# States of two convolutions stored value by value from their channel layout, instead of through transpositions and row transfers

## The chip, the cores and the metric

The kernel runs on one core of a Trainium2 chip. The time is that of one execution on the device in microseconds (us), as the median of three runs. A core has five engines that run side by side, each with its own queue of instructions: TensorE (PE: matrix products and transpositions, results in PSUM), VectorE (DVE), ScalarE (ACT), GpSimd (POOL) and SyncE (SP). ACT, POOL and SP also issue transfers between SBUF and DRAM; 16 DMA engines carry them out. The rows call the queue of SP's transfers q1, that of ACT's q10 and that of POOL's q0. The engines wait for each other by semaphores: a counter that one raises and another waits for.

## The reference

One step of a hybrid decoder layer for two groups of tokens: a prompt (1 sequence of 1024 tokens) and samples (8 sequences of 4 tokens), D_MODEL = 1024, branch width W = 512. What matters here is what two causal convolutions leave behind as their new state:

```python
def causal_dwconv(x, hist, w):
    k = w.shape[0]
    xp = jnp.concatenate([hist.astype(x.dtype), x], axis=1)
    y = lax.conv_general_dilated(xp, w[:, None, :], window_strides=(1,), padding='VALID', ...)
    return y, xp[:, -(k - 1):]

a = a_val * jax.nn.sigmoid(a_gt)
a, new_hist_a = causal_dwconv(a, hist_a, a_dw_w)          # k = 31: 30 rows
ch, new_hist_c = causal_dwconv(c_c * c_h, hist_c, c_conv_w)  # k = 3: 2 rows
```

The outputs touched are new_conv_a_prompt (30 rows of 512 values), new_conv_c_prompt (2 rows of 512), new_conv_a_sample (8 sequences of 30 rows: 26 rows are the old state moved up by 4, and 4 are new) and new_conv_c_sample (8 sequences of 2 rows). All values are 4-byte floats. The rest (three mixers, gates, an output projection, a mixture of 32 experts) is unchanged.

## The kernel before

The prompt is worked in two halves of 512 tokens, g = 0 and g = 1; the 32 sample tokens ride with g = 1 (so 544 columns). Channels lie on the 128 partitions: W = 512 channels are CW = 4 chunks, D_MODEL = 1024 are KD = 8 chunks. A product is an "item": the weight tile of 128 output channels against all tokens, as three products of rounded high parts and low rests (`item`, L2612 to L2614), with g = 1 in two column parts of 272. Items alternate between the PSUM tiles z[0] and z[1].

For each item SP loads the weights into one of WS = 5 buffers (L1308), ACT writes the high part (`w_round`, L1577) and DVE the rest (`w_low`, L1865), AHEAD = 3 items ahead of PE. Everything is written out by hand: each engine's order is the order of the code in its block.

The stretch around the change, in g = 1: after the items of the mixers come 8 pairs of items for the gates of branch C ("GC"), 8 for branch B ("GB") and 8 for branch A ("GA"). A pair is a gate item into z[0] and a branch item into z[1]. ACT takes the sigmoid of z[0] into `sig` (`gate`, L1755) and then rounds two weight tiles; DVE multiplies z[1] by `sig` into `macc`, and between these it does the steps of the convolution over `conv` (L2034), which are all done before the pair GB 3. PE may write z[0] anew when ACT's sigmoid has read it, and z[1] when DVE has multiplied it.

The last rows of the convolutions' inputs are kept by DVE in `a_tail` (128 partitions x 4 chunks x (30 + 32) values: 30 prompt positions, then 8 sequences of 4) and `p_tail` (2 + 32 values), with the channel on the partition. DVE wrote the last of them by 617.1 us, before GC begins. In the outputs the channel is the fastest index, so one partition's values lie 2048 bytes apart in DRAM. Before, they get there like this, all in g = 1:

- PE, after the item GB 0 of h: `states` transposes chunk by chunk into the PSUM tiles q[0] ("stA") and q[1] ("stC"), 16 transpositions (L2503), then `factor_columns` ("mc") transposes `bn_g` into q[0], for which ACT must have read stA.
- ACT, after its four roundings `act1_hi`: four copies out of q into `p_in`, `cv`, `ot[0]`, `ot[1]` (L1773, L1774).
- POOL: a DRAM-to-DRAM transfer of the 26 old rows (L1505), then it waits until ACT has read both, and issues 18 row transfers (L1508 to L1512), each row of 2048 bytes in one piece. Behind them in its queue are the loads of `xres` (L1517).

`st_out` counts these transfers; ACT waits for all of them before its first output item, because `ot` is then overwritten, and POOL before it loads rows into `xA` and `xs_s` (L1532).

Of the kernel before, what the change touches and what calls it, by code (L numbers as in the profile page):

```python
# [80 lines left out]
def build(nc, x_prompt, x_sample, c_prompt, c_sample, state_conv_a, state_conv_c, norm1_g, norm2_g,  # L81
# [5 lines left out]
    with ctx:  # L87
# [375 lines left out]
        def use(s, *name):  # L463
            QFILL[name], QUSE[name] = (s, qn[s]), (s, qf[s])
            qn[s] += 1
            qf[s] += name[0] not in ("ada", "rows")
# [9 lines left out]
        for g in range(2):  # L476
            if g:
                for i in range(PT):
                    use(0, "h2T", 0, i)
            for i in range(CW):  # L480
                use(0, "vT", g, i)
            for t in range(PT + g):
                use(t % 2, "sp", g, t)
            if g:
                use(0, "stA"), use(1, "stC"), use(0, "mc"), use(1, "sc")
            for c in range(CW):
                use(c % 2, "mu", g, c)
            use(1, "var", g)
            if g:
                use(0, "sr")  # L490
            for c in range(CW):
                use(c % 2, "bc", g, c)
            if g == 0:
                for t in range(PT + 1):
                    use(t % 2, "xT", 1, t)
            else:
                use(1, "rank0")
            for n in range(KD):
                use(n % 2, "oT", g, n)
# [211 lines left out]
        def moe_gpsimd(pool):  # L711
# [59 lines left out]
                    pool.wait_ge(m_y, n_)  # L771
                    scatter_dma(0, xcol[:, 0:1], o_sc)

            pool.wait_ge(st_out, 16 * (3 + 2 * NS))

        def step_T(pe, b, s):

# [581 lines left out]
        def _(pool):  # L1359
# [138 lines left out]
            for g in range(2):  # L1498
                if g == 1:

                    pool.wait_ge(vn_ok, 2 * PT + 1)
                    pool.dma_start(new_v_sample[0].rearrange("n t c -> (n t) c"), v_tok[0:SMP, PT, :]).then_inc(v_out, 16)
                    pool.dma_start(bn_g[:, 0:P], modc_dram[0:P, :]).then_inc(mc_in, 16)
                    pool.dma_start(bn_g[0:2 * KD, P:2 * P], modc_dram[P:9 * 2 * KD, :]).then_inc(mc_in, 16)
                    pool.dma_start(new_a_sample[0, :, 0:HA - TS, :], state_conv_a[0, :, TS:HA, :]).then_inc(st_out, 16)  # L1505
                    q_wait_read(pool, "stA")
                    q_wait_read(pool, "stC")
                    pool.dma_start(new_a_prompt[0, 0], p_in[0:HA, 0:W]).then_inc(st_out, 16)  # L1508
                    pool.dma_start(new_c_prompt[0, 0], ot[0][0:HC, 0:W]).then_inc(st_out, 16)
                    for n in range(NS):  # L1510
                        pool.dma_start(new_a_sample[0, n, HA - TS:HA, :], cv[n * TS:(n + 1) * TS, 0:W]).then_inc(st_out, 16)
                        pool.dma_start(new_c_sample[0, n], ot[1][n * TS + TS - HC:(n + 1) * TS, 0:W]).then_inc(st_out, 16)  # L1512
                    pool.wait_ge(v_out, 16)

                pool.wait_ge(blo_ok, CW * (g + 1))
# [10 lines left out]
                pool.dma_start(A2[:], mod_dram[0:1, 4 * D:5 * D].to_broadcast([P, D])).then_inc(ab_in, 16)  # L1526
                if g:
                    pool.wait_ge(alo_ok, 2 * CW)
                    pool.wait_ge(st_out, 16 * (3 + 2 * NS))
                    for k, off in enumerate((3, 4)):  # L1530
                        for n in range(NS):
                            pool.dma_start(xs_s[n * TS:(n + 1) * TS, :] if k else xA[SMP + n * TS:SMP + (n + 1) * TS, PT, :],  # L1532
                                           mod_dram[1 + n:2 + n, off * D:(off + 1) * D].to_broadcast([TS, D])
                                           ).then_inc(abs_in, 16)
# [8 lines left out]
        def _(act):  # L1543
# [129 lines left out]
            for g in range(2):  # L1673
# [72 lines left out]
                for i in range(CW):  # L1746
                    b_chunk(i)


                def gate(n0, i):  # L1750

# [6 lines left out]

                for i in range(KD):
                    gate(GC0, i)  # L1760

                if g == 0:
                    for s in range(2):
# [3 lines left out]
                act.wait_ge(bb_ok, PT + g * (PT + 1))  # L1767
                for c in range(CW):
                    act.activation(act1_hi[:, c, 0:T], u_sb[:, c, 0:T], ACT.Copy).then_inc(bhi_ok, 1)
                if g:  # L1770
                    for k, rows in ((0, HA), (1, HC)):
                        s = q_wait_ready(act, ("stA", "stC")[k])
                        act.activation((p_in, ot[0])[k][0:rows, 0:W], q[s][0:rows, 0, :], ACT.Copy)  # L1773
                        act.activation((cv, ot[1])[k][0:SMP, 0:W], q[s][0:SMP, 1, :], ACT.Copy).then_inc(q_free[s], 1)  # L1774

                def squares(cs):

# [51 lines left out]

                macc_high(KD - 1)  # L1830
                if g:
                    act.wait_ge(st_out, 16 * (3 + 2 * NS))
                for j in range(KD // 2):
                    for s in range(2):
                        if g == 0:
# [663 lines left out]
        def _(pe):  # L2499
# [236 lines left out]
            for g in range(2):  # L2736
# [77 lines left out]
                        spatial(PT, SMP)  # L2814
                    pairs(GC0, i, i + 1, act0_hi, act0_lo)

                def states():
                    for name, src, n in (("stA", a_tail, HA), ("stC", p_tail, HC)):
                        s = q_wait_free(pe, name)
                        for c in range(CW):  # L2820
                            transposed(q[s][0:n, 0, c * P:(c + 1) * P], src[:, c, 0:n])
                            last = transposed(q[s][0:SMP, 1, c * P:(c + 1) * P], src[:, c, n:n + SMP])
                        last.then_inc(q_ready[s], 1)

                def mean(c):
                    s = q_wait_free(pe, "mu", g, c)
                    pe.wait_ge(cnv_ok, g + 1)
# [24 lines left out]

                item(g, GB0, h_hi, h_lo)
                if g:
                    states()
                    factor_columns()
                item(g, GB0 + 1, act1_hi, act1_lo, split_ok=blo_ok)
                pairs(GB0, 1, 3, act1_hi, act1_lo)
# [87 lines left out]
```

## Time and profile before

| | |
|---|---|
| median of 3 runs | 1657.01 us (1656.86 to 1657.71) |
| profiled execution | 1660.13 us, of it span 1658.4 us |
| PE busy | 1584.3 us, 96% of the span |
| DVE, ACT, POOL busy | 1244.5, 808.0, 226.4 us |
| granted PE clock | 0.982 of full over the span |

The span runs from the first to the last recorded instruction. "Busy" sums the instructions of an engine; register, semaphore and DMA-issuing instructions are not counted as busy. A row of the timeline has the start in us, the duration in us (of all instructions merged in it), the engine, the line in the kernel, the operation, the output and input by name, their shapes, the count, and in brackets how long the engine sat idle before it and who released it. ACTq, SPq and POOLq are the parts of these engines that issue transfers.

### The profile page before, as it was taken

How to read it: one execution, taken by the hardware profiler on the slowest of the kernel's cores; microseconds unless marked ns; L12 is line 12 of the kernel's file. 1: busy time of each engine (PE TensorE's matmuls, PEld its weight loads, DVE VectorE, ACT ScalarE, POOL GpSimd, SP SyncE). 2: the span in 40 equal slices, each digit the busy share in tenths (PEclk: the TensorE clock that was granted, in tenths of full speed). 3: DMA queues.
4: the chain of work that ended last, by engine and by line, in shares of the span. 5: the costliest groups of instructions: out<-in, count | busy, mean ns of one | idle time of the engine just before them, and what ended most of it. 6: DMA issues, size and time to landing. Idle time of an engine off the chain costs nothing.

```text
span 1658.4 us, 23365 instructions
## 1 busy us (share of the span) xinstructions
PE 1584.3 (96%) x9186; PEld 1353.4 (82%) x9186; DVE 1244.5 (75%) x1685; ACT 808.0 (49%) x877; POOL 226.4 (14%) x238
## 2 busy tenths in 40 slices
PE   5999999999999999999999989999999999999953
PEld 3777788788789999999999968888888888888841
DVE  4668886746838898877455468898898898898838
ACT  4222232234323213223142367788788788788722
POOL 3310000000000000002000204433212112112100
PEclk9999999999999999999899999999999999999987
DMA  9965222424435222234123648999999999999864
GB/s 341 311 193 167 85 84 83 146 75 143 126 89 168 87 83 81 77 91 135 58 77 102 223 185 302 412 400 395 392 385 377 380 375 383 376 390 396 297 242 179
DMA packets 215984, 368.65 MB, mean 222 GB/s; under 512 B 15266, under 2 KB 163826, under 8 KB 190522
## 3 DMA queue, kind: packets, MB, share of 16 engines
q1 hardware_dynamic: 198972, 332.41, 56.5%
q0 software_dynamic: 16256, 32.58, 5.6%
q10 hardware_dynamic: 646, 2.15, 0.3%
q8 instruction: 74, 1.21, 0.3%
q14 instruction: 36, 0.29, 0.0%
HBM read 353.59 MB, written 31.27 MB: 232 GB/s over the span
## 4 chain that ended last, share of the span: by engine, by line
PE 86%; DVE 8%; DVEq 2%; DMA 2%; issue 1%; ACT 1%; POOL 0%; SPq 0%; POOLq 0%; ACTq 0%
PE z L2612 15%; PE z L2614 15%; PE z L2613 15%; PE z L791 7%; PE z L789 7%; PE z L790 7%; PE z L806 4%; PE z L807 4%; PE z L808 4%; PE q L780 2%; PE q L2503 1%; DMA ada_h<-in_w_ada_dram 1%; PE q L2522 1%; PE q L797 1%; DVE conv L2034 1%
## 5 line engine op out<-in xcount | busy, mean ns | idle before, releaser
L1113 DVE TENSOR_TENSOR wl<-wr,whr 128x2048 fp32r<-128x2048 f32 x198 | 444.0, 2284 | 0.0
L2612 PE MATMUL z<-h_hi,w_hi 128*128 128x272 f32 (+1 forms) x1248 | 409.7, 328 | 3.5 <-DVE h_lo L1865 2.4
L2614 PE MATMUL z<-h_hi,w_lo 128*128 128x272 f32 (+1 forms) x1248 | 404.2, 324 | 0.0
L2613 PE MATMUL z<-h_lo,w_hi 128*128 128x272 f32 (+1 forms) x1248 | 403.3, 323 | 0.0
L952 ACT ACTIVATE whr<-wr 128x2048 fp32r<-128x2048 f32 x198 | 376.3, 1914 | 31.2 <-PE z L791 30.0
L1865 DVE TENSOR_TENSOR w_lo<-w_raw,w_hi 128x1024 fp32r<-128x1024 f32 (+1 forms) x168 | 179.4, 1068 | 135.3 <-ACT w_hi L1577 135.1
L2612 PEld LDWEIGHTS z<-h_hi,w_hi 128*128 128x128 f32 x1248 | 236.3, 189 | 33.7 <-issue 13.4
L2614 PEld LDWEIGHTS z<-h_hi,w_lo 128*128 128x128 f32 x1248 | 236.0, 189 | 17.0
L2613 PEld LDWEIGHTS z<-h_lo,w_hi 128*128 128x128 f32 x1248 | 236.4, 189 | 15.5 <-issue 0.2
L789 PE MATMUL z<-whr,xTh 128*128 128x512 f32 x528 | 208.8, 396 | 0.1
L791 PE MATMUL z<-wl,xTh 128*128 128x512 f32 x528 | 206.1, 390 | 0.0
L790 PE MATMUL z<-whr,xTl 128*128 128x512 f32 x528 | 205.5, 389 | 0.0
L2034 DVE SCALAR_TENSOR_TENSOR conv<-a_in,parT,conv 128x512 f32<-128x512 f32 x360 | 193.7, 582 | 14.1 <-issue 0.9
L1577 ACT ACTIVATE w_hi<-w_raw 128x1024 fp32r<-128x1024 f32 (+1 forms) x168 | 150.4, 929 | 45.0 <-DMA w_raw<-in_w_in_dram 44.9
L1755 ACT ACTIVATE sig<-z 128x512 f32<-128x512 f32 (+1 forms) x48 | 29.3, 611 | 293.4 <-PE z L2614 293.4
L733 POOL DMA_INDIRECT y_rows<-ysb,tb x32 | 78.1, 2442 | 410.9 <-ACT ysb L944 410.9
L791 PEld LDWEIGHTS z<-wl,xTh 128*128 128x128 f32 x528 | 99.1, 188 | 21.2
L789 PEld LDWEIGHTS z<-whr,xTh 128*128 128x128 f32 x528 | 99.6, 189 | 19.8 <-DVE xTl L1113 0.3
L790 PEld LDWEIGHTS z<-whr,xTl 128*128 128x128 f32 x528 | 99.3, 188 | 19.6
L806 PE MATMUL z<-whr,gTh 128*128 128x512 f32 x264 | 105.8, 401 | 0.6 <-DVE gTl L1113 0.6
L808 PE MATMUL z<-wl,gTh 128*128 128x512 f32 x264 | 103.1, 390 | 0.0
L807 PE MATMUL z<-whr,gTl 128*128 128x512 f32 x264 | 103.0, 390 | 0.0
(431 smaller groups left out, 2172.9 us busy)
## 6 DMA issues: line engine op xcount, KB each, us to landing
wr<-in_w_dram SPq DMA_DIRECT2D x198, 1024.0 KB, 9.6
w_raw<-in_w_in_dram SPq DMA_DIRECT2D x104, 512.0 KB, 3.8
ada<-in_w_ada_dram SPq DMA_DIRECT2D x6, 2048.0 KB, 14.1
w_raw<-in_w_branch_dram SPq DMA_DIRECT2D x48, 256.0 KB, 2.7
w_raw<-in_w_out_dram SPq DMA_DIRECT2D x16, 512.0 KB, 4.0
yin<-y_rows SPq DMA_DIRECT2D x16, 512.0 KB, 9.4
ada_h<-in_w_ada_dram SPq DMA_DIRECT2D x2, 2048.0 KB, 15.1
ada_u<-in_w_ada_dram SPq DMA_DIRECT2D x2, 2048.0 KB, 9.8
```

Source lines behind the costliest of these rows:

```text
L789: pe.matmul(out, xTh[s][:, k, :], hi[:, i * FF:(i + 1) * FF], start=(k == 0), stop=False)
L790: pe.matmul(out, xTl[s][:, k, :], hi[:, i * FF:(i + 1) * FF], start=False, stop=False)
L791: last = pe.matmul(out, xTh[s][:, k, :], lo[:, i * FF:(i + 1) * FF], start=False, stop=(k == KD - 1))
L806: pe.matmul(out, gTh[:, k, :], hi[:, w0:w0 + 512], start=(k == 0), stop=False)
L808: last = pe.matmul(out, gTh[:, k, :], lo[:, w0:w0 + 512], start=False, stop=(k == KF - 1))
L952: act.activation(whr[n % HN][:], wr[n % RN][:], ACT.Copy).then_inc(m_hi, 1)
L1113: return dve.tensor_tensor(out, a, b, op)
L1865: return dve.tensor_tensor(out, a, b, op)
L2034: last = dve.scalar_tensor_tensor(out, x, wt, out, ALU.mult, ALU.add)
L2612: pe.matmul(out, w_hi[w][:, k, :], hi[:, k, t0:t1], start=(k == 0), stop=False)
L2613: pe.matmul(out, w_hi[w][:, k, :], lo[:, k, t0:t1], start=False, stop=False)
L2614: last = pe.matmul(out, w_lo[w][:, k, :], hi[:, k, t0:t1], start=False, stop=(k == kn - 1))
```

## The change

The 16 transpositions of PE, the four copies of ACT and POOL's 19 transfers are left out, with the two uses of the q tiles. Instead ACT issues transfers straight from `a_tail` and `p_tail`, one chunk of 128 channels after each of the gates GC 0 to GC 3, with patterns in which every value of 4 bytes goes to its own place in DRAM. The old rows' DRAM-to-DRAM transfer goes to ACT too. `st_out` counts 33 transfers instead of 19; its two waits stay.

```diff
@@ the table of the uses of the q tiles @@
             if g:
-                use(0, "stA"), use(1, "stC"), use(0, "mc"), use(1, "sc")
+                use(0, "mc"), use(1, "sc")
@@ POOL, g == 1 @@
                     pool.dma_start(bn_g[0:2 * KD, P:2 * P], modc_dram[P:9 * 2 * KD, :]).then_inc(mc_in, 16)
-                    pool.dma_start(new_a_sample[0, :, 0:HA - TS, :], state_conv_a[0, :, TS:HA, :]).then_inc(st_out, 16)
-                    q_wait_read(pool, "stA")
-                    q_wait_read(pool, "stC")
-                    pool.dma_start(new_a_prompt[0, 0], p_in[0:HA, 0:W]).then_inc(st_out, 16)
-                    pool.dma_start(new_c_prompt[0, 0], ot[0][0:HC, 0:W]).then_inc(st_out, 16)
-                    for n in range(NS):
-                        pool.dma_start(new_a_sample[0, n, HA - TS:HA, :], cv[n * TS:(n + 1) * TS, 0:W]).then_inc(st_out, 16)
-                        pool.dma_start(new_c_sample[0, n], ot[1][n * TS + TS - HC:(n + 1) * TS, 0:W]).then_inc(st_out, 16)
                     pool.wait_ge(v_out, 16)
@@ ACT @@
+                def states(c):
+                    cc = slice(c * P, (c + 1) * P)
+
+                    def state(dst, src):
+                        act.dma_start(dst, src, allow_slow_non_contiguous=True).then_inc(st_out, 16)
+
+                    if c == 0:
+                        act.dma_start(new_a_sample[0, :, 0:HA - TS, :], state_conv_a[0, :, TS:HA, :]).then_inc(st_out, 16)
+                    state(new_a_prompt[0, 0, :, cc].rearrange("h p -> p h"), a_tail[:, c, 0:HA])
+                    state(new_c_prompt[0, 0, :, cc].rearrange("h p -> p h"), p_tail[:, c, 0:HC])
+                    for t in range(TS):
+                        state(new_a_sample[0, :, HA - TS + t, cc].rearrange("n p -> p n"), seqs(a_tail[:, c, HA:HA + SMP])[:, :, t])
+                    for t in range(HC):
+                        state(new_c_sample[0, :, t, cc].rearrange("n p -> p n"),
+                              seqs(p_tail[:, c, HC:HC + SMP])[:, :, TS - HC + t])
...
                 for i in range(KD):
                     gate(GC0, i)
+                    if g and i < CW:
+                        states(i)
...
-                if g:
-                    for k, rows in ((0, HA), (1, HC)):
-                        s = q_wait_ready(act, ("stA", "stC")[k])
-                        act.activation((p_in, ot[0])[k][0:rows, 0:W], q[s][0:rows, 0, :], ACT.Copy)
-                        act.activation((cv, ot[1])[k][0:SMP, 0:W], q[s][0:SMP, 1, :], ACT.Copy).then_inc(q_free[s], 1)
...
                 if g:
-                    act.wait_ge(st_out, 16 * (3 + 2 * NS))
+                    act.wait_ge(st_out, 16 * (1 + 8 * CW))
@@ PE @@
-                def states():
-                    for name, src, n in (("stA", a_tail, HA), ("stC", p_tail, HC)):
-                        s = q_wait_free(pe, name)
-                        for c in range(CW):
-                            transposed(q[s][0:n, 0, c * P:(c + 1) * P], src[:, c, 0:n])
-                            last = transposed(q[s][0:SMP, 1, c * P:(c + 1) * P], src[:, c, n:n + SMP])
-                        last.then_inc(q_ready[s], 1)
...
                 item(g, GB0, h_hi, h_lo)
                 if g:
-                    states()
                     factor_columns()
                 item(g, GB0 + 1, act1_hi, act1_lo, split_ok=blo_ok)
```

The order of PE before, at the end of the gate item GB 0 in g = 1 (the first column is the instruction's place in PE's row, w_hi and w_lo are the weights' parts):

```order
3852 L2614 MATMUL z<-h_hi_65,w_lo_89 128x272
3853 L2503 MATMUL q<-ident,a_tail 30x128 [waits q_free0]
3854 L2503 MATMUL q<-ident,a_tail 32x128
...
3861 L2503 MATMUL q<-ident,p_tail 2x128 [waits q_free1]
3862 L2503 MATMUL q<-ident,p_tail 32x128
...
3869 L2503 MATMUL q<-ident,bn_g 128x128 [waits mc_in,q_free0]
3870 L2503 MATMUL q<-ident,bn_g 128x16
3871 L2612 MATMUL z<-act_hi_78,w_hi_100 128x272 [waits blo_ok,z_free1,wlo_ok]
```

And now, at the same place:

```order
3852 L2619 MATMUL z<-h_hi_65,w_lo_89 128x272
3853 L2508 MATMUL q<-ident,bn_g 128x128 [waits mc_in,q_free0]
3854 L2508 MATMUL q<-ident,bn_g 128x16
3855 L2617 MATMUL z<-act_hi_78,w_hi_100 128x272 [waits blo_ok,z_free1,wlo_ok]
3856 L2618 MATMUL z<-act_lo_80,w_hi_100 128x272
```

The 16 transpositions from `a_tail` and `p_tail` are gone, and `bn_g` follows the gate item at once; the wait for q_free0 is now for an earlier reader of q[0].

ACT's order before, from the gate GC 0 to GC 2 in g = 1:

```order
285 L1755 ACTIVATE sig<-z 128x544 [waits z_free1,item_mm]
286 L1577 ACTIVATE w_hi_96<-w_raw_91 128x512 [waits w_in0]
287 L1577 ACTIVATE w_hi_97<-w_raw_92 128x1024 [waits w_in1]
288 L1755 ACTIVATE sig<-z 128x544 [waits z_free1,item_mm]
289 L1577 ACTIVATE w_hi_98<-w_raw_93 128x512 [waits w_in2]
290 L1577 ACTIVATE w_hi_99<-w_raw_94 128x1024 [waits w_in3]
```

And now:

```order
285 L1763 ACTIVATE sig<-z 128x544 [waits z_free1,item_mm]
286 L1569 ACTIVATE w_hi_96<-w_raw_91 128x512 [waits w_in0]
287 L1569 ACTIVATE w_hi_97<-w_raw_92 128x1024 [waits w_in1]
288 L1748 DMA out_dram<-in_state_conv_a_dram 8x13312
289 L1745 DMA out_dram<-a_tail 128x30x1
290 L1745 DMA out_dram<-p_tail 128x2x1
291 L1745 DMA out_dram<-a_tail 128x8x1 x4
292 L1745 DMA out_dram<-p_tail 128x8x1 x2
293 L1763 ACTIVATE sig<-z 128x544 [waits z_free1,item_mm]
294 L1569 ACTIVATE w_hi_98<-w_raw_93 128x512 [waits w_in2]
295 L1569 ACTIVATE w_hi_99<-w_raw_94 128x1024 [waits w_in3]
296 L1745 DMA out_dram<-a_tail 128x30x1
```

Nine transfers stand between the sigmoids of GC 0 and GC 1, and eight after each of GC 1, GC 2 and GC 3. None of them waits for a semaphore. POOL's order loses the rows between the load of `bn_g` and the loads of `xres`.

## Rows read from the trace of the kernel before

**Rows 1.** The page: busy time and share of PE, and the chain's shares by engine.
```profile
PE 1584.3 (96%) x9186; PEld 1353.4 (82%) x9186; DVE 1244.5 (75%) x1685; ACT 808.0 (49%) x877; POOL 226.4 (14%) x238
...
PE 86%; DVE 8%; DVEq 2%; DMA 2%; issue 1%; ACT 1%; POOL 0%; SPq 0%; POOLq 0%; ACTq 0%
```

**Rows 2.** Busy by stage: PE, PEld, DVE, ACT, POOL, clock, DMA share, GB/s.
```profile
676.00:712.00 36.00, 34.60 (x299) 33.88 (x298) 33.41 (x73) 8.36 (x12) 2.10 (x4) 1.00 0.32 93
712.00:732.00 20.00, 20.00 (x178) 19.49 (x177) 14.53 (x26) 4.18 (x6) 0.00 (x0) 1.00 0.26 75
...
760.00:800.00 40.00, 40.00 (x312) 37.91 (x311) 29.90 (x57) 7.35 (x11) 11.19 (x23) 1.00 0.45 133
```

**Rows 3.** Timeline of PE at the transpositions.
```profile
755.91 1.03 PE L2503 MATMUL q<-ident,a_tail 128*30 128x128 f32 x8
756.78 1.04 PE L2503 MATMUL q<-ident,p_tail 128*2 128x128 f32 x8
758.10 0.49 PE L2503 MATMUL q<-ident,bn_g 128*128 128x128 f32 x2 [0.28 <-ACT cv L1774]
```

**Rows 4.** Timeline of ACT and DVE from 753 to 787 us, and PE's first mean.
```profile
756.98 0.59 ACT L1773 ACTIVATE p_in<-q 30x512 f32<-30x512 f32 x1 [5.63 <-PE q L2503]
...
758.90 0.60 ACT L1755 ACTIVATE sig<-z 128x544 f32<-128x544 f32 x1
...
753.93 2.62 DVE L1865 TENSOR_TENSOR act_lo<-u_sb,act_hi 128x544 fp32r<-128x544 f32 x4
...
776.26 6.85 DVE L2034 SCALAR_TENSOR_TENSOR conv<-a_in,parT,conv 128x512 f32<-128x512 f32 x14
...
786.71 0.86 PE q L2828 x2
```

**Rows 5.** Timeline of ACT at the gates GC 0 to GC 4.
```profile
676.96 0.63 ACT L1755 ACTIVATE sig<-z 128x544 f32<-128x544 f32 x1 [2.92 <-PE z L2614]
677.48 1.57 ACT L1577 ACTIVATE w_hi<-w_raw 128x512 fp32r<-128x512 f32 x2
686.03 0.62 ACT L1755 ACTIVATE sig<-z 128x544 f32<-128x544 f32 x1 [6.97 <-PE z L2614]
...
717.95 0.62 ACT L1755 ACTIVATE sig<-z 128x544 f32<-128x544 f32 x1 [9.65 <-PE z L2614]
```

**Rows 6.** Timeline of PE: the first product of the gate item GC 2.
```profile
688.85 0.29 PE L2612 MATMUL z<-h_hi,w_hi 128*128 128x272 f32 x1
```

**Rows 7.** Timeline of DVE: the product that needs the sigmoid of GC 1.
```profile
693.62 0.71 DVE L1865 TENSOR_TENSOR macc<-z,sig 128x544 f32<-128x544 f32 x1
```

**Rows 8.** Timeline: transfers issued by ACT and SP in the first 22 us.
```profile
2.06 0.35 ACTq L1548 DMA_DIRECT2D badaR<-in_b_ada_dram  x1
...
0.81 1.08 SPq L1319 DMA_DIRECT2D ada_h<-in_w_ada_dram  x2
1.94 14.16 SPq L1319 DMA_DIRECT2D ada<-in_w_ada_dram  x2
```

**Rows 9.** SP's queue from 0 to 16.1 us: packets, MB, share of 16 engines.
```profile
q1 hardware_dynamic: 1545, 3.13, 55.1%
```

**Rows 10.** The same from 640 to 680 us.
```profile
q1 hardware_dynamic: 5744, 2.88, 25.4%
```

**Rows 11.** The same from 1200 to 1240 us, in the experts' stage.
```profile
q1 hardware_dynamic: 1955, 14.24, 91.3%
```

**Rows 12.** POOL's queue from 1016 to 1024 us, with 4-byte writes of slot_table.
```profile
q0 software_dynamic: 144, 0.10, 3.9%
```

**Rows 13.** Issues of the page: KB each, median us to landing.
```profile
rb<-in_b_router_e_dram POOLq DMA_DIRECT2D x1, 16.0 KB, 6.7
...
rw<-in_w_router_e_dram POOLq DMA_DIRECT2D x1, 128.0 KB, 8.5
```

**Rows 14.** Timeline of POOL: the last of its transfers before, and what stood behind.
```profile
759.57 0.55 POOL L1508 DMA_DIRECT2D out_dram<-p_in  x1 [51.05 <-ACT ot L1774]
...
768.54 2.14 POOL L1517 DMA_DIRECT2D xres<-in_x_prompt_dram  x4
```

More of the change, by code:

```diff
@@ L772, in moe_gpsimd @@
                     scatter_dma(0, xcol[:, 0:1], o_sc)
-            pool.wait_ge(st_out, 16 * (3 + 2 * NS))
+            pool.wait_ge(st_out, 16 * (1 + 8 * CW))
         def step_T(pe, b, s):
@@ L1528, in _ @@
                     pool.wait_ge(alo_ok, 2 * CW)
-                    pool.wait_ge(st_out, 16 * (3 + 2 * NS))
+                    pool.wait_ge(st_out, 16 * (1 + 8 * CW))
                     for k, off in enumerate((3, 4)):
```

## The prediction, on record before the changed kernel ran

> **What bounds the kernel now.** I read the page's busy times and chain first. PE is busy 96% of the span, and 86% of the chain that ended last is PE, 8% DVE [rows 1]. So what leaves PE's row counts in full wherever PE is the engine waited for, and what is put on ACT costs nothing until PE or DVE waits for it. Next the busy times by stage: from 760 to 800 us PE is busy 40.00 of 40.00 us with DVE at 29.90, so just behind the removed work PE sets the pace; from 676 to 712 us, where the new work goes, DVE has 33.41 of 36 and PE 34.60, so there both are tight and ACT, with 8.36, is nearly empty [rows 2]. Then the timeline of PE at the transpositions and of ACT at the gates, and last the DMA queues, for what a small piece costs.
>
> **What goes.** PE's 16 transpositions start at 755.91 us, and bn_g, which stands behind them, at 758.10, after 0.28 us of idle time for ACT's copy cv [rows 3]. Without them bn_g starts at 755.91: 758.10 - 755.91 = 2.19 us off PE. What could be late there instead? The next item wants DVE's act_lo, four subtractions that begin at 753.93 and take 2.62 us, so the last is done at 756.55 [rows 4]. The item would begin some 0.45 us after 755.91, and wants the four one after the other, the first of which is done at about 753.93 + 2.62 / 4 = 754.6; it is covered. The sigmoid of GB 0 waited behind the four copies until 758.90; it can now run at about 755.9, and the roundings behind it start sooner too. Behind that, the one place where PE waits on DVE's backlog would be the means, which want the end of the convolution: its last row ends at 776.26 + 6.85 = 783.11 and PE's first mean starts at 786.71; 3.6 us of slack, more than the 2.19 [rows 4]. DVE starts its 16 steps sooner as well, for they are behind the multiplication that PE releases. So -2.19 us stays. After 800 us PE's row goes on without gaps (96% over the whole span), and the experts' stage begins when the dense part is done: it moves forward with it.
>
> POOL loses 18 row transfers and the wait of 51.05 us before them [rows 14]. Behind them are the loads of xres, which can now start when act_lo is done, at about 756.6 instead of 768.54. They are wanted only by the output items, 16 pairs later; their 2 MB meet the weight loads 12 us sooner than before, which are three items ahead. Nothing, either way.
>
> **What comes.** Count the pieces first. For one chunk of 128 channels: 128 x 30 (prompt a) + 128 x 2 (prompt c) + 4 x 128 x 8 (samples a) + 2 x 128 x 8 (samples c) = 10240 values, each a piece of its own of 4 bytes. Over 16 DMA engines that is 640 pieces each, and 2560 for all four chunks. In bytes it is nothing (0.16 MB); the pieces are the price.
>
> Issuing: a small transfer took ACT 0.35 us [rows 8]. Chunk 0 has nine: 3.2 us. ACT has done its two roundings at 677.48 + 1.57 = 679.05 and idles 6.97 us until the sigmoid of GC 1 at 686.03 [rows 5]. That fits, if issuing is all.
>
> It is not all if the queue fills up. SP shows it: two transfers ada_h were issued in 1.08 us, the next two took 14.16 us [rows 8]. Each is 2048 KB in pieces of 2 KB, 1024 pieces or 64 per DMA engine, so at 16.10 us four times 64 = 256 per engine had been taken, and 1545 / 16 = 97 were done [rows 9]. A queue thus holds about 160 pieces per DMA engine, and the engine that issues stands still while it is full. ACT then stands for (640 - 160) times the time t of one piece in chunk 0, and for all four chunks the last issue returns at 679.5 + 2400 t, as long as the queue never runs dry.
>
> When does PE feel it? The sigmoid of GC 1 reads z[0], which PE writes again from 688.85 us [rows 6]. It takes 0.62 us, so ACT must be back by 688.2: t up to 18 ns. DVE's product with that sigmoid starts only at 693.62 [rows 7]. Over all four chunks the mark is the sigmoid of GC 4, which started at 717.95; with the same slack of about 2.4 us it may start at 720.4. 679.5 + 2400 t = 720.4 gives t = 17 ns. Up to there the change costs nothing, above it 2.4 us per ns.
>
> **What is t?** No row shows a long run of 4-byte pieces, so I bound it. From below: SP's weight pieces of 512 bytes took 25.4% of 16 x 40 us over 5744 packets, 28.3 ns each [rows 10]. In the experts' stage, with pieces of 8 KB, 14.24 MB took 91.3% of 640 us, 41 us per MB, which is 21 ns for 512 bytes [rows 11]. So a packet has some 7 ns beside its bytes, and a 4-byte one costs 7 to 8 ns. POOL's queue agrees: 144 packets, most of them 4-byte writes into slot_table in DRAM, took 3.9% of 128 us = 5.0 us, of which 0.10 MB at 41 us is 4.1, leaving about 6 ns a packet [rows 12]. From above, by the nearest row: the weights' 28.3 ns, if small pieces are fed or written no faster than these. From the far side: rw, 1024 pieces of 128 bytes or 64 per engine, landed in 8.5 us, 1.8 us more than the 16 KB of rb just before [rows 13], again 28 ns; were its whole landing time pieces, 133 ns. I take 8 ns, the one that 4-byte packets themselves show: a chunk is 5.1 us of DMA time, and as (640 - 160) x 8 ns = 3.8 us ACT is back by about 683.5, 2.5 us before the sigmoid wants it. The weight loads share the DMA engines, which are busy 0.32 there [rows 2], and get 0.5 us longer (64 x 8 ns), far inside three items of lead.
>
> The writes of slot_table show 4-byte pieces into DRAM at the price of any small packet. The Trainium skill ("DMA: Bandwidth & Descriptors", Specifications and Rules for kernel authors) says that a strided last dimension becomes one descriptor per element, and that pieces under 512 B make the DMA do a read-modify-write. By that second rule each piece might count twice, 16 ns, and the last issue would return at 679.5 + 38.4 = 717.9, still inside the limit; the first rule is the count that I use.
>
> **Sum.** -2.19 (PE) + 0 (ACT, covered) + 0 (POOL, DMA) = -2.2 us. The profiled execution took 1660.13 us (span 1658.4, 1.7 around it) and would take 1657.9. It was 3.1 us above the median of the runs; against the median of 1657.01 the forecast is 1654.8 us, 0.13% less. What a measurement of this kernel tells from no change is about 0.2%, 3.3 us: the forecast is inside it.
>
> **Rivals.**
> A, the queue is full and ACT stands. Place: between the sigmoids of GC 0 and GC 4. It decides from t = 17 ns; the 0.2% are passed at 679.5 + 2400 t = 725.9, t = 19.3 ns. With 28.3 ns the last issue returns at 747.4, the sigmoid of GC 4 is 27.0 us late, and the time is 1657.0 + 27.0 - 2.2 = 1681.8. For it: SP stood 14.16 us for just such a reason, 10240 pieces are ten times what any one transfer of this kernel has, and the only small pieces in long runs are at 28 ns. Against it: those are 512 bytes each, and the 4-byte packets show 6 to 8 ns.
> B, the same with a much higher price: 4-byte writes 2048 bytes apart go slower than anything seen here. At 60 ns the last issue returns at 823.5 and the time is 1657.0 + 103.1 - 2.2 = 1757.9; at 133 ns it would be 998.7 and 1933. Only the landing times of rw speak for it.
> C, the 2.19 us are given back: DVE or the weights are late at some place behind 760 us, and the time is 1657.0. For it: DVE's slack at the means is only 3.6 us. Against it: PE has no gap there and DVE waits for PE, not the reverse.
> D, more than 3.3 us come back, because ACT's earlier roundings and POOL's earlier loads help later: 1653. No wait of PE in the rows stands for it.
>
> **Chances.** The forecast 0.44 (own range 1654.0 to 1656.3); C 0.08; D 0.06; A 0.28, of which 0.04 ends within 0.2% (t between 17 and 19 ns); B 0.14. So faster by over 0.2%: 0.06. Within 0.2%: 0.44 + 0.08 + 0.04 = 0.56. Slower: 0.24 + 0.14 = 0.38. The range leaves out most of D below and the dearest of A and all of B above: 1653.6 to 1705, the upper end being 38 ns per piece (679.5 + 91.2 = 770.7, 50.3 us late, less 2.2).
>
> **What would show it.** Right: bn_g's transposition follows the gate item within 0.1 us; the rows of ACTq with a_tail are together under 6 us per chunk; the sigmoids keep their distances of 9.07 us from GC 0 to GC 1 and 31.92 us from there to GC 4, with ACT idle before each; queue q10 shows some 41,000 more packets. Wrong: single issues of a_tail that take several us, ACT idle before the sigmoids gone, and PE waiting for ACT's sigmoid at the gate items GC 2 to GC 5; then t is (the last issue's return - 679.5) / 2400, whatever the packet times say. If PE loses no time there and the whole is still not about 2 us shorter, the step on the slack behind 760 us is the wrong one.

## The result, and the profile after

| | before | after |
|---|---|---|
| median | 1657.36 us (4 runs, 1656.86 to 1658.09) | 1828.61 us (4 runs, 1825.26 to 1832.93) |
| ratio, 95% interval | | 1.1029 (1.1015 to 1.1043) |
| profiled execution, span | 1660.13, 1658.4 us | 1832.93, 1831.2 us |
| granted PE clock over the span | 0.982 | 0.937 |

The change makes the kernel 10.3% slower: 171.3 us. The forecast was 1654.8 us and the range ended at 1705. So the forecast was wrong by 173.8 us. It went the way of rivals A and B (a full queue, ACT standing, PE waiting for its sigmoid), at a price per piece between B's two. One execution can come out some per cent slower than the next of the same kernel; where that happened (two of the four runs of experiment 2, one of the four of experiment 7) the whole range is given, and what is said holds for the faster ones too.

The page of the changed kernel; what answers to [rows 1], and the queue of ACT's transfers:

```profile
PE 1588.8 (87%) x9170; PEld 1358.6 (74%) x9170; DVE 1245.8 (68%) x1685; ACT 806.2 (44%) x873; POOL 215.4 (12%) x219
...
q10 hardware_dynamic: 42134, 2.74, 10.4%
...
PE 77%; ACTq 11%; DVE 5%; DMA 2%; issue 1%; DVEq 1%; ACT 1%; POOL 0%; SPq 0%; POOLq 0%
```

PE's work is nearly the same (1588.8 us busy against 1584.3); its share falls because the span grows. Queue q10 had 646 packets in the kernel before and has 42134 now: the 40,960 pieces and the old rows. In the chain ACTq, the issuing part of ACT, has risen from 0% to 11%. A reader should look there first: 11% of 1831 us is some 200 us in which nothing but an issue stood on the path that set the end.

ACT's timeline at the gates GC 0 to GC 4, which answers to [rows 5]:

```profile
679.25 0.62 ACT L1763 ACTIVATE sig<-z 128x544 f32<-128x544 f32 x1 [2.92 <-PE z L2619]
679.26 0.79 ACTq L1748 DMA_DIRECT2D out_dram<-in_state_conv_a_dram  x1
...
680.09 0.45 ACTq L1745 DMA_DIRECT2D out_dram<-a_tail  x1
...
680.57 11.16 ACTq L1745 DMA_DIRECT2D out_dram<-p_tail  x1
691.76 33.54 ACTq L1745 DMA_DIRECT2D out_dram<-a_tail  x4
725.33 12.39 ACTq L1745 DMA_DIRECT2D out_dram<-p_tail  x2
737.82 0.62 ACT L1763 ACTIVATE sig<-z 128x544 f32<-128x544 f32 x1 [56.48 <-issue]
...
788.08 0.63 ACT L1763 ACTIVATE sig<-z 128x544 f32<-128x544 f32 x1 [48.17 <-issue]
...
845.21 0.62 ACT L1763 ACTIVATE sig<-z 128x544 f32<-128x544 f32 x1 [55.04 <-issue]
...
897.81 0.62 ACT L1763 ACTIVATE sig<-z 128x544 f32<-128x544 f32 x1 [50.51 <-issue]
```

The first big transfer (30 values on 128 partitions, 240 pieces per DMA engine) takes 0.45 us in its row, close to the 0.35 us of [rows 8]. The next one has 16 pieces per DMA engine and takes 11.16 us. So the row that is long is not the one whose pieces are many, but the one that finds the queue full. The idle times before the four sigmoids sum to 210.2 us. Before the change they were idle time that ended when PE was done; now they end by "issue".

The waits from 676 to 900 us:

```profile
DVE w_lo L1870 <- ACT w_hi L1569: 177.8, 5, 47.8
...
PE z L2617 <- ACT sig L1763: 170.1, 4, 47.3
```

170.1 us of PE's waiting in four pieces is the loss, but for 1.2 us. The busy times by stage (columns as in [rows 2]):

```profile
680.00:720.00 40.00, 11.31 (x90) 11.08 (x89) 13.72 (x37) 1.35 (x2) 0.00 (x0) 0.67 1.39 50
...
760.00:800.00 40.00, 11.15 (x74) 11.02 (x76) 8.80 (x15) 2.09 (x3) 1.58 (x3) 0.59 1.35 23
800.00:840.00 40.00, 0.95 (x16) 0.71 (x14) 0.00 (x0) 0.00 (x0) 0.00 (x0) 0.54 1.02 21
...
900.00:960.00 60.00, 60.00 (x490) 59.44 (x489) 44.60 (x83) 15.07 (x22) 2.62 (x5) 0.98 0.64 117
```

PE is busy 49.9 of the 220 us from 680 to 900, and 60.00 of the 60 us behind them. The DMA share passes 1 (1.39), so the recorded times of the packets overlap, and the time of a packet is not yet the pace of a queue. Last, the queues from 680 to 860 us, with the landing times of the weights:

```profile
q10 hardware_dynamic: 33499, 0.56, 80.9%
q1 hardware_dynamic: 6272, 3.15, 39.0%
...
w_raw<-in_w_in_dram SPq DMA_DIRECT2D x5, 512.0 KB, 36.2
```

A packet of q10 is recorded with 0.809 x 16 x 180 / 33499 = 70 ns, where I had taken 8. A packet of SP's weights in the same time has 0.390 x 2880 / 6272 = 179 ns, against 28.3 from [rows 10], and a weight tile lands 36.2 us after its issue. So beside the small writes the weights of another queue come late too.

### The profile page after: what moved, and what is told of

Its sections match the earlier page's. It is cut to its first block, busy times and chain, and to the rows that moved or that the text cites. A ratio compares the mean times of both kernels' runs of the same rounds, so it can differ in the third digit from the quotient of the medians.

```text
span 1831.2 us, 23342 instructions
## 1 busy us (share of the span) xinstructions
PE 1588.8 (87%) x9170; PEld 1358.6 (74%) x9170; DVE 1245.8 (68%) x1685; ACT 806.2 (44%) x873; POOL 215.4 (12%) x219
## 3 DMA queue, kind: packets, MB, share of 16 engines
q10 hardware_dynamic: 42134, 2.74, 10.4%
## 4 chain that ended last, share of the span: by engine, by line
PE 77%; ACTq 11%; DVE 5%; DMA 2%; issue 1%; DVEq 1%; ACT 1%; POOL 0%; SPq 0%; POOLq 0%
PE z L2617 14%; PE z L2619 14%; PE z L2618 13%; ACTq L1745 11%; PE z L791 6%; PE z L789 6%; PE z L790 6%; PE z L806 3%; PE z L808 3%; PE z L807 3%; PE q L780 2%; PE q L2508 1%; DMA ada_h<-in_w_ada_dram 1%; PE q L2527 1%; PE q L797 1%
## 5 line engine op out<-in xcount | busy, mean ns | idle before, releaser
L2617 PE MATMUL z<-h_hi,w_hi 128*128 128x272 f32 (+1 forms) x1248 | 412.8, 331 | 173.5 <-ACT sig L1763 170.1
L808 PE MATMUL z<-wl,gTh 128*128 128x512 f32 x264 | 103.1, 391 | 0.0
```

What stands on the lines that cost most here:

```text
L2617: pe.matmul(out, w_hi[w][:, k, :], hi[:, k, t0:t1], start=(k == 0), stop=False)
```

## The experiments

All are edits of the changed kernel. Experiments 1, 2 and 7 were run 11, 4 and 4 times, the others once each. The theory after the result: each small write is dear at its destination, the queue is full, ACT stands (S), and the DMA engines are also clogged for others (M).

**1. What the states' writes cost in all.** They are left unwritten, but for the old rows, which POOL moves:

```diff
-                    if g and i < CW:
-                        states(i)
```

> The states of the prompt and the 4 new rows and 2 rows of the samples are not written at all; the transfer of the 26 old rows is back on POOL. What is left of the change is what it removes. My step on PE's 16 transpositions says 2.2 us less than the kernel before, 1655.1, ratio 0.9987. The rival that the gap is given back later says 1657.4, ratio 1.0000. Nothing of the 171 us may be left in it: if it were slower than before, the loss would not come from the transfers.

Measured over 11 runs: 1657.08 us, ratio 0.9996 (0.9987 to 1.0005), against 1657.89 of the kernel before on the same chip. So all of the 171 us is in ACT's transfers. What any way of writing the states could win over the kernel before is 0.8 us by the medians, 2.2 us at the lower end of the interval, and 0 lies inside it. The timelines of PE and ACT at the removed transpositions, which answer to [rows 3]:

```profile
755.73 0.29 PE L2618 MATMUL z<-h_hi,w_lo 128*128 128x272 f32 x1
755.86 0.43 PE L2507 MATMUL q<-ident,bn_g 128*128 128x128 f32 x2
```
```profile
756.06 0.63 ACT L1764 ACTIVATE sig<-z 128x544 f32<-128x544 f32 x1 [4.76 <-PE z L2618]
765.58 0.63 ACT L1764 ACTIVATE sig<-z 128x544 f32<-128x544 f32 x1 [7.43 <-PE z L2618]
```

bn_g comes right behind the gate item, 2.24 us before its time in the kernel before, where GB 1 had its sigmoid at 767.88: 2.30 us gained there. In the end the span is 3.7 us shorter in the two profiled executions and 0.8 us in the medians. The profiled one of before is 2.8 us above that kernel's median and had a granted clock of 0.87 from 800 to 840 us against 0.96 here, so the 2.3 us are measured at the place and not in the total. They are still there behind PE's means, the place that the prediction feared. Kernel before, then this one:

```profile
800.12 0.62 ACT L1755 ACTIVATE sig<-z 128x544 f32<-128x544 f32 x1 [11.28 <-PE z L2614]
```
```profile
797.82 0.63 ACT L1764 ACTIVATE sig<-z 128x544 f32<-128x544 f32 x1 [11.28 <-PE z L2618]
```

**2. Whose instruction stands.** POOL, which nobody waits for there, issues the same transfers at 709 us:

```diff
@@ POOL; the same function as ACT had @@
+                        def state(dst, src):
+                            pool.dma_start(dst, src, allow_slow_non_contiguous=True).then_inc(st_out, 16)
...
+                    for c in range(CW):
+                        states(c)
```

> The same 32 transfers of 4-byte pieces, issued by POOL behind bn_g (at about 710 us) instead of by ACT between its sigmoids. Theory S (ACT stands in its queue and PE waits for its sigmoid; the pieces by themselves disturb little): 1655 to 1662 us, ACT idle before each sigmoid as in the kernel before. Theory M (the pieces clog the DMA engines, the weights' loads come late and PE starves whoever issues): as slow as the change or nearly, 1750 us or more, with ACT's w_hi waiting for DMA w_raw. In between, some 1680 us, both.

Measured: 1845.88 us (median of 4 runs, 1819.91 to 1867.67; the two faster ones 1819.91 and 1841.86). The waits from 700 to 900 us:

```profile
POOL out_dram L1509 <- issue: 166.6, 2, 85.3
...
ACT w_hi L1587 <- DMA w_raw<-in_w_branch_dram: 78.9, 2, 71.3
ACT w_hi L1587 <- DMA w_raw<-in_w_in_dram: 64.3, 5, 56.5
```

POOL now does the standing and ACT waits for no issue, but the weights come late instead: they land 68.5 us after their issue from 700 to 860 us, against 3.8 us in the kernel before (680 to 960 us). The time is no better. S alone is false: moving the transfers off the critical engine saves nothing, because PE then waits for engines that wait for weights. Nor is the price one of ACT's queue: from POOL's first state transfer (709.30 us) to the end of its last issue (906.39) lie 197 us, and fewer than 2560 pieces per DMA engine were done in them, so a piece took at least 77 ns here.

The packet counts of the two pages, experiment 1's first, hold a trap:

```profile
q0 software_dynamic: 15680, 32.41, 5.5%
```
```profile
q0 software_dynamic: 16896, 32.58, 10.7%
```

POOL's queue shows 1216 more packets for 40,960 pieces, where ACT's queue showed one for each. On POOL's queue a count of packets is not a count of pieces.

**3. The same number of pieces, spread out.** Every value goes to a place of its own in a scratch tensor, the channels 20 KB apart and the values of one channel 128 to 512 bytes; the states' outputs are not written:

```diff
-                    state(new_a_prompt[0, 0, :, cc].rearrange("h p -> p h"), a_tail[:, c, 0:HA])
+                    sp_ = spread_dram[cc, :, 0:1].rearrange("p h o -> p (h o)")
+                    state(sp_[:, 0:HA], a_tail[:, c, 0:HA])
```

> Same pieces, same issuer, same places in ACT's order, but each value goes to a place of its own in a DRAM scratch tensor, 128 bytes or more from any other (the outputs are not written). In the change 16 neighbouring channels, from four DMA engines, write into the same 64 bytes. Theory W (each partial write into DRAM costs what it costs): still 85 to 90 ns per piece and DMA engine, 1820 to 1830 us. Theory N (the neighbours' writes collide): t falls to 10 to 30 ns, 1655 to 1690 us.

Measured: 1684.91 us. 40,960 writes of 4 bytes, as many as in the changed kernel, and 144 us less. Theory W falls, N stands.

**4. The same pieces as reads**, from the old states in DRAM into `ot[0]` (states' outputs not written):

```diff
-                    state(new_a_prompt[0, 0, :, cc].rearrange("h p -> p h"), a_tail[:, c, 0:HA])
+                    state(ot[0][:, 80 * c:80 * c + HA], state_conv_a[0, 0, :, cc].rearrange("h p -> p h"))
```

> Same number of 4-byte pieces with the same distances, but read from DRAM into SBUF instead of written into DRAM (the outputs are not written). Theories W and N (the write into DRAM is what is dear): t of 8 to 30 ns, ACT hardly stands, 1655 to 1690 us. Theory G (making or handling so many descriptors is dear, whatever the direction): t stays at 85 to 90 ns, 1820 to 1830 us.

Measured: 1668.13 us. The queue from 680 to 760 us:

```profile
q10 hardware_dynamic: 41097, 0.16, 27.9%
```

A packet takes 0.279 x 1280 / 41097 = 8.7 ns, almost exactly the 8 ns that I had taken from [rows 10 to 12]. (They are all done by 735 us; to there they keep the DMA engines busy for 40.6%.) Theory G falls. Still ACT stands, and its four chunks pass at 21 ns a piece. So even where the writes are no trouble, the queue moves at more than twice the packet's own time. The packet time of the profile is not the queue's rate.

**5. How far apart is far enough?** Scratch tensors with 64 or 32 bytes for each value (neighbouring channels that far apart, rows 32 or 16 KB):

```diff
+        apart_dram = nc.dram_tensor("apart", (80, W, 16), F32, kind="Internal").ap()
...
+                        return apart_dram[r0:r0 + n, cc, 0:1].rearrange("h p o -> p (h o)")
```

> The states go to a scratch tensor in DRAM where every value has 64 bytes of its own (neighbouring channels 64 bytes apart, rows 32 KB apart) instead of to the outputs (4 bytes and 2 KB apart); count, order and places of issue are as in the changed kernel. So the states' outputs are not written. With values at least 512 bytes apart the same 40,960 writes had given 1684.9 us (29 ns per piece of a DMA engine), in the outputs 1828.6 us (90 ns). Theory N, neighbouring channels' writes disturb each other only inside one small place of DRAM (64 bytes or less): 25 to 35 ns, 1675 to 1700 us. Rival, the place is larger (a whole 512-byte or 2-KB stretch) or it is the distance of the rows: 70 to 95 ns, 1780 to 1840 us.

> As the one with 64 bytes, but with 32 bytes for each value (rows 16 KB apart). The states' outputs are not written. If two values in one 64-byte place are what costs, this one is dearer than its sister: 35 to 60 ns, 1700 to 1760 us, since only two values share a place and not sixteen. If the place is 32 bytes or less: the same time as with 64 bytes within 5 us. If the distance has to be several hundred bytes: both near 1830 us.

Measured: 1679.00 us with 64 bytes and 1712.54 with 32. With 64 bytes to itself a write costs no more than with 128 and more (what the first of these two expectations calls 512 bytes is 128 at the least); where two values share 64 bytes it costs more. The rows' distance differs too, 32 KB and 16 KB, so this pair alone doesn't show that it is the sharing.

**6. Who shares the place?** The rows of one channel 8 bytes apart, so that eight values share 64 bytes, all from one partition; then the same with the channels 20 KB instead of 640 bytes apart (states' outputs not written in either):

```diff
+        rows_dram = nc.dram_tensor("byrow", (W, 80, 2), F32, kind="Internal").ap()
...
+                        return rows_dram[cc, r0:r0 + n, 0:1].rearrange("p h o -> p (h o)")
```
```diff
-        rows_dram = nc.dram_tensor("byrow", (W, 80, 2), F32, kind="Internal").ap()
+        rows_dram = nc.dram_tensor("byrow", (W, 2560, 2), F32, kind="Internal").ap()
```

> Count, order and places of issue as in the changed kernel; the states go to a scratch tensor in which the values of one channel lie 8 bytes apart (every second place of 4 bytes) and the channels 640 bytes apart. So eight values share 64 bytes of DRAM, but all eight come from the same partition and the same transfer or one just behind it. The states' outputs are not written. Theory P, any sharing of 64 bytes costs, since each small write must read and put back the place: as dear as the outputs or nearly, 60 to 90 ns per piece, 1755 to 1830 us. Theory N, only places shared by neighbouring partitions cost, because different DMA engines work on them at the same time: 25 to 32 ns, 1675 to 1692 us, as with 64 or 512 bytes between values.

> As the kernel with the rows 8 bytes apart (1756.9 us; 57 ns per piece of a DMA engine between its sigmoids of GC 1 and GC 4), but with the channels 20 KB apart instead of 640 bytes, so that the whole scratch is 10 MB and not 0.3 MB. Still eight values share 64 bytes of DRAM. The states' outputs are not written. Of the layouts measured so far the dearer one is always both the one in which more values share 64 bytes and the one with the smaller whole extent (0.16 MB: 83 ns, 0.3 MB: 57 ns, 1.3 MB: 38 ns, 2.6 MB: 23 ns, 10 MB: 28 ns). Theory P, writes into the same 64 bytes disturb each other: unchanged, 50 to 65 ns and 1740 to 1770 us. Rival, the extent decides, since a small one lies in few parts of the memory: 23 to 30 ns and 1675 to 1690 us.

Measured: 1756.89 us, and 1804.14 us with the channels further apart. It isn't only neighbouring partitions that disturb each other (theory N of the first run falls), and a small extent is not the reason: the rival in the second expectation wanted 1675 to 1690 us. The second kernel and experiment 3 are the cleanest pair: channels 20 KB apart in a scratch of 10 MB in both, and only the distance within a channel goes from 128 to 512 bytes down to 8, for 119 us more. That the larger distance of the channels makes it dearer, which no theory here foresaw, is not shown: the two runs are 47 us apart, and four runs of one kernel were 48 us apart in experiment 2 and 33 in experiment 7.

The timelines give t in two ways. With the prediction's formula, from the sigmoids of GC 0 and GC 4, t = (GC 4 - GC 0 - 2.54) / 2400 (2.54 is 679.5 - 676.96 of [rows 5]). And from GC 1 to GC 4, three chunks of 640 pieces, which needs no assumption on the queue's depth. The last column is the prediction's sum with the measured GC 4: 1657.4 - 2.2 + (GC 4 - GC 0 - 43.44), where 43.44 is the limit 720.4 less 676.96.

| kernel | values in 64 bytes | GC 0, GC 1, GC 4 (us) | t, formula | t, GC 1 to 4 | measured | sum |
|---|---|---|---|---|---|---|
| reads | - | 675.75, 690.16, 729.35 | 21 ns | 20 ns | 1668.1 | 1665.4 |
| 64 bytes apart | 1 | 679.22, 697.44, 741.80 | 25 | 23 | 1679.0 | 1674.3 |
| 128 to 512 bytes apart | 1 | 677.07, 695.12, 749.80 | 29 | 28 | 1684.9 | 1684.5 |
| 32 bytes apart | 2 | 677.74, 704.60, 777.05 | 40 | 38 | 1712.5 | 1711.1 |
| rows 8 bytes apart | 8 | 675.73, 707.48, 817.86 | 58 | 57 | 1756.9 | 1753.9 |
| the same, channels wide apart | 8 | 677.08, 724.25, 868.09 | 79 | 75 | 1804.1 | 1802.8 |
| the outputs (the change) | 16 | 679.25, 737.82, 897.81 | 90 | 83 | 1828.6 | 1830.3 |

The sum hits every one of the seven times within 5 us, over a loss of 11 to 171 us. It starts from the measured GC 4, so what it tests is the last step: ACT's lateness behind the limit goes into the time one for one, and t is what differs. The rows behind two of the columns, of the 64-byte kernel and of the wide one:

```profile
741.80 0.62 ACT L1764 ACTIVATE sig<-z 128x544 f32<-128x544 f32 x1 [12.03 <-issue]
748.88 0.63 ACT L1764 ACTIVATE sig<-z 128x544 f32<-128x544 f32 x1 [4.99 <-PE z L2620]
```
```profile
868.09 0.62 ACT L1764 ACTIVATE sig<-z 128x544 f32<-128x544 f32 x1 [43.79 <-issue]
877.08 0.62 ACT L1764 ACTIVATE sig<-z 128x544 f32<-128x544 f32 x1 [6.90 <-PE z L2620]
```

In both, the first sigmoid after the last transfers is again one that PE ends.

**7. Can spacing save it?** All of the change's writes, to the real outputs, in 44 transfers of at most 64 pieces per DMA engine, two behind each gate from GC 0 on (and one transfer for the old rows first):

```diff
+                def some_states(n):
+                    if g:
+                        for _ in range(min(n, len(moves))):
+                            state(*moves.pop(0))
...
                 for i in range(KD):
                     gate(GC0, i)
-                    if g and i < CW:
-                        states(i)
+                    some_states(2)
```

> The whole of the change's writes, to the real outputs, but in 45 transfers of at most 64 pieces per DMA engine, two behind each of the gates and the convolution's rows of ACT from GC 0 on (to about 900 us), so that the queue is seldom full and ACT seldom stands. Theory S, the loss is ACT standing at a full queue: then at 90 ns a piece two transfers are 5.8 to 11.5 us of queue against 9 us per pair of items, ACT stands little, 1660 to 1690 us. Theory M, the writes also clog the DMA engines for the weight loads, whoever issues them and when: 40,960 writes cost the same DMA time, the weights come late wherever they are, 1700 to 1830 us.

Measured: 1774.79 us (median of 4 runs, 1770.38 to 1803.49), ratio 1.0699 (1.0677 to 1.072). Its waits and queues from about 680 to 960 us:

```profile
DVE w_lo L1881 <- ACT w_hi L1569: 113.7, 20, 11.6
ACT w_hi L1569 <- DMA w_raw<-in_w_in_dram: 107.6, 14, 14.5
...
PE z L2628 <- ACT sig L1768: 14.5, 5, 5.6
```
```profile
q1 hardware_dynamic: 28504, 14.30, 68.0%
...
w_raw<-in_w_in_dram SPq DMA_DIRECT2D x19, 512.0 KB, 19.0
w_raw<-in_w_branch_dram SPq DMA_DIRECT2D x19, 256.0 KB, 15.9
```

ACT stands much less now (to 960 us PE waits 14.5 us for its sigmoids, not 170.1), and 54 us come back. The other 117 us remain. What holds ACT up now is the weights: their packets take 0.680 x 16 x 280 / 28504 = 107 ns each, a tile lands after 19.0 us, and ACT waits 107.6 us for them. The page, and the busy times by stage:

```profile
PE 1612.0 (91%) x9170; PEld 1377.9 (78%) x9170; DVE 1246.0 (70%) x1685; ACT 809.4 (46%) x873; POOL 215.6 (12%) x219
```
```profile
680.00:700.00 20.00, 17.64 (x148) 17.43 (x148) 11.66 (x28) 1.26 (x2) 0.00 (x0) 1.00 1.17 27
700.00:960.00 260.00, 200.98 (x1468) 193.10 (x1465) 116.05 (x223) 53.64 (x75) 4.21 (x8) 0.86 0.98 63
960.00:1000.00 40.00, 29.74 (x205) 29.20 (x204) 14.26 (x34) 7.72 (x11) 0.00 (x0) 0.83 1.24 62
1000.00:1020.00 20.00, 15.65 (x106) 15.46 (x105) 8.41 (x14) 4.44 (x6) 1.07 (x2) 0.83 1.05 81
1020.00:1080.00 60.00, 51.40 (x399) 51.09 (x398) 22.02 (x44) 23.19 (x92) 8.02 (x16) 0.91 0.51 150
```

PE stands 84.6 of these 400 us (in the kernel before 1.7 of the 280 us from 680 to 960), waiting in turn for ACT and DVE, which wait for the weights. In these stretches with their many pauses the granted clock is 0.83 to 0.91 from 700 us on, and PE's busy time in all is 27.7 us above that of [rows 1]. Over the whole span PE stands 156.6 us against 74.1. These 82.5 and the 27.7 are the 110.2 us between the two profiled spans (1768.6 and 1658.4). Taking away the standing of ACT uncovers the second cost of the same writes.

**8. One chunk alone.** Only chunk 0 and the old rows are written (`if g and i < 1`):

> Only chunk 0 of the states (640 of the 2560 pieces per DMA engine) and the old rows are written, by ACT after the gate GC 0; chunks 1 to 3 are left unwritten. By the formula with 90 ns and 160 pieces held by the queue ACT is back at 679.3 + 480 x 0.090 = 722.5 us, and the sigmoid of GC 1, which had to be there at about 690.5, is 32 us late: 1657.4 + 32 - 2.2 = 1687 us. If the first chunk costs what the trace of the changed kernel shows (sigmoid of GC 1 at 737.8, 47 us late), 1702 us. If only the sum of four chunks overloads something and one alone goes at 29 ns or less, under 1662 us.

Measured: 1712.04 us. ACT's timeline and the waits:

```profile
678.53 17.22 ACTq L1745 DMA_DIRECT2D out_dram<-p_tail  x1
695.77 35.81 ACTq L1745 DMA_DIRECT2D out_dram<-a_tail  x4
731.61 11.65 ACTq L1745 DMA_DIRECT2D out_dram<-p_tail  x2
743.37 0.62 ACT L1763 ACTIVATE sig<-z 128x544 f32<-128x544 f32 x1 [64.06 <-issue]
```
```profile
PE z L2617 <- ACT sig L1763: 54.9, 1, 54.9
```

The price is not one that only four chunks together reach: a chunk is as dear alone, with 54.9 us of waiting where the longest single wait of the changed kernel was 47.3. Both of my numbers were low, the one by the formula (1687) because (743.37 - 677.21 - 2.54) / 480 is 133 ns, not 90. In the changed kernel the same chunk gives 117 ns (ACT is back after 58.6 us there and after 66.2 us here), so the formula makes a first chunk dearer than those behind it.

## Why the prediction was wrong

**The step that failed is "What is t?"**, where I took 8 ns out of bounds of 7 to 133. It measured 90 by the same formula. The term "+0 (ACT, covered)" is 175.1 us: the sigmoid of GC 4 came at 897.81, and its limit is 679.25 + 43.44 = 722.69. Then 1657.4 + 175.1 - 2.2 = 1830.3 against 1828.6 measured. Three things were wrong in that step, of different size:

- *The recorded time of a packet was taken for the rate of the queue.* Experiment 4 has packets of 8.7 ns and a queue that moves at 21 ns. That alone passes the limit of 17 ns and gives 1668. The 28.3 ns, which I had as the upper bound "by the nearest row" and set aside, was the value for pieces that don't share: 25 and 29 ns were measured, and rival A's 1681.8 us stands between 1679.0 and 1684.9.
- *A read's price was taken for a write's, and a lone write's for a crowd's.* The 4-byte writes of [rows 12] were at most 144 packets in 8 us, into slot_table, and their 6 ns were again a recorded time and no pace. Nothing in the trace of before had thousands of writes that share places of 64 bytes, which the layout of the outputs makes of them: neighbouring channels are neighbouring 4-byte values, and 16 of them are 64 bytes. That is the step from 25 to 90 ns. The diff and the output's shape showed the sharing; I counted pieces and did not ask where they land.
- *The upper end was named and then not used.* 133 ns, "were its whole landing time pieces", had "only the landing times of rw" for it. The truth was nearer to it than to my value. With ends 19 times apart, a value at the very bottom needed a row of the same kind, and there was none.

The Trainium skill ("DMA: Bandwidth & Descriptors", Specifications) gives a read-modify-write for pieces under 512 B. I had worked out 16 ns from it, "each piece might count twice". The runs agree with the direction, in that writes are dearer than reads and dearer still where they share a place, and not with that estimate: 23 to 28 ns against 20 without sharing and up to 83 with it. Since the price rises from 64 to 32 bytes between values and not from 128 to 64, the 512 bytes of the page are not the size of the place in which small writes disturb each other here.

**Queue depth.** I had about 160 pieces per DMA engine from SP's start. In the changed kernel 9 transfers, 10240 + 528 packets, had been issued at 737.82 us and 8982 packets recorded by 737; the last issue returned by 897.8 with 1508 packets to come. That is 94 to 112 per DMA engine on average. The order of size was right, and in a sum of 2560 pieces the difference is 2%; for one chunk it is more, which may be a part of why the expectation for experiment 8 was low. Whether the fullest of the 16 holds 160 can't be told from these records.

**The 2.19 us of PE** are right at their place: in the changed kernel too bn_g follows the gate item at once (934.17, the product ahead of it starts at 934.05), and 2.24 to 2.30 us were gained in experiment 1. In the total the ratio of experiment 1 leaves everything between a gain of 2.2 and a loss of 0.8 us (0.9987 and 1.0005 of 1657.9), so what becomes of them later stays open. Rival C named the means as the place where they might be given back, and there they are not: 2.30 us are left at 800 us, in one execution of each kernel. My step on the slack at the means was not what failed.

**The weight loads** I had 0.5 us longer per chunk. They landed after 36.2 us, against 3.8. In the changed kernel this cost little more, as PE stood for ACT anyway; experiments 2 and 7 uncover it. The Trainium skill ("DMA: Bandwidth & Descriptors", Back-pressure in remote DMA) says for transfers to another core that stalled writes stall the other queues of the same DMA engine too. This case shows the like with writes to DRAM on one core: SP's packets went from 28.3 to 107 and 179 ns beside them. That it is the same mechanism is not shown.

**Rivals.** A and B had the mechanism, place, limit and the way to the time: 103.1 us late at 60 ns in B, and the kernel with rows 8 bytes apart has 98.7 (817.86 - 675.73 - 43.44) at 58 ns. Their chances, 0.42 together, were too low only because t was pinned; the range should have gone to B's prices. As the two ends of t gave 1654.8 and 1933, an upper end at 1705 was not what the bounds made it.

**The clock** went down with PE's waiting: granted 0.67, 0.59 and 0.54 of full in the stretches above, that is between the levels of 1.2 and 2.4 GHz, and products of 128x272 took 0.43 us instead of 0.29 from 738.95 to 741.67 us, behind a pause of 47.28 us. From 900 to 960 us it is 0.98.

```profile
738.59 0.56 PE L2617 MATMUL z<-h_hi,w_hi 128*128 128x272 f32 x1 [47.28 <-ACT sig L1763]
738.95 0.43 PE L2618 MATMUL z<-h_lo,w_hi 128*128 128x272 f32 x1
...
741.83 0.29 PE L2619 MATMUL z<-h_hi,w_lo 128*128 128x272 f32 x1
```
In this kernel the slow products lay in stretches that ACT's standing set anyway, so they are no term of their own.

## What to carry to other kernels

A transfer whose innermost step isn't contiguous was priced here by its pieces and by where they land, not by its bytes and not by the recorded time of a packet: look at how many pieces share 64 bytes of DRAM, and count 20 to 30 ns per piece of a DMA engine at best and three to four times that in a dense output. Such a transfer has two costs, the issuing engine that stands once the queue is full and the loads of all others that come late; moving it to an idle engine or spacing it takes away the first alone (nothing gained with POOL, 54 of 171 us with spacing). 16 transpositions of 2.2 us and row transfers of 2048 bytes were the cheap way, and nothing that writes the states another way can win more than about 2 us here.

## What the runs showed of the hardware that was not expected

- 4-byte pieces over 16 DMA engines, issued by ACT: 20 ns per piece of an engine as reads, 23 to 28 as writes each in 64 bytes of their own, 38 with two in 64 bytes, 57 to 75 with eight, 83 with sixteen (GC 1 to GC 4).
- Reads of 4 bytes had packets of 8.7 ns in a queue that moved at 20: while they ran (680 to 735 us) they kept the DMA engines busy for 40.6%.
- POOL's queue recorded 1216 packets for 40,960 pieces of 4 bytes, ACT's queue one for each.
- With eight values in 64 bytes, one run with the channels 20 KB apart gave 75 ns and one with 640 bytes gave 57; whether that is more than the scatter of such kernels is open. What in the memory makes shared places dear was not looked into either: only that it goes with the sharing.
